# Routing and gathering from the centred input, with the later places made inside the first expert slot

## The reference, cut to what matters

```python
y = jnp.concatenate([mix, xa], -1) @ w_out[i]          # sparse or latent attention, and cross-attention
x = layer_norm(DEEPNORM_ALPHA * x + y, ln_g[i, 0], ln_b[i, 0])
f = hier_moe(x, ...)
x = layer_norm(DEEPNORM_ALPHA * x + f, ln_g[i, 1], ln_b[i, 1])

def layer_norm(x, g, b):
    mu = mean(x); var = mean(square(x - mu))
    return (x - mu) * rsqrt(var + LN_EPS) * g + b

def hier_moe(xs, ...):        # 4 groups of 4 experts, 512 hidden features each
    pg = softmax(xs @ w_grp + b_grp)              # the best group
    le = (xs @ w_exp + b_exp) of that group       # its 4 experts, softmax, the best two
    hdn = silu(xs @ w_gate[e]) * (xs @ w_up[e]) * gate[e]
    return sum over e of hdn @ w_down[e]
```

## Time and profile before

| | |
|---|---|
| median of 3 executions | 2118.57 us (2117.32 to 2120.0) |
| profiled execution | 2114.99 us, span 2113.2 us |
| granted PE clock, mean | 0.996 |
| PE, DVE, ACT busy | 97%, 69%, 53% of the span |

### The profile page before, as it was taken

The page is one execution under the profiler, slowest core; times in us unless marked ns, Lnnn a source line. Parts: engine busy times, 40 slices in busy tenths (PEclk is TensorE's granted clock), DMA queues, the critical chain, the costliest instruction groups (busy, mean ns, idle before and its releaser), DMA issues. The chain is left out here.

```text
span 2113.2 us, 34585 instructions
## 1 busy us (share of the span) xinstructions
PE 2044.1 (97%) x14050; PEld 1853.5 (88%) x14050; DVE 1464.0 (69%) x2157; ACT 1114.7 (53%) x1580; POOL 26.3 (1%) x35
## 2 busy tenths in 40 slices
PE   7999999999999999989999989999999889999998
PEld 7999997999999998879999967888888758888886
DVE  5666785666666665576665477788987466888896
ACT  4333733544343445574333456677775455776774
POOL 1000000000000020000000000000000000000000
PEclk9999999999999999999999999999999999999999
DMA  9555322655545543435553532589985514789992
GB/s 310 186 186 184 123 89 92 211 185 186 186 148 185 185 146 100 154 124 189 186 184 124 156 123 100 204 323 368 351 328 207 220 40 160 271 328 337 343 359 93
DMA packets 246671, 421.44 MB, mean 199 GB/s; under 512 B 7716, under 2 KB 135104, under 8 KB 246432
## 3 DMA queue, kind: packets, MB, share of 16 engines
q1 hardware_dynamic: 245632, 418.09, 56.2%
q0 software_dynamic: 544, 1.62, 0.2%
q10 hardware_dynamic: 384, 0.21, 0.1%
HBM read 416.70 MB, written 1.05 MB: 198 GB/s over the span
## 5 line engine op out<-in xcount | busy, mean ns | idle before, releaser
L662 PE MATMUL banks<-x_hi,w_hi 128*128 128x256 f32 x1360 | 385.8, 284 | 0.0
L663 PE MATMUL banks<-x_lo,w_hi 128*128 128x256 f32 x1360 | 384.9, 283 | 0.0
L664 PE MATMUL banks<-x_hi,w_lo 128*128 128x256 f32 x1360 | 384.8, 283 | 0.0
L3318 DVE TENSOR_TENSOR w_lo<-weight_ring,w_hi 128x1024 fp32r<-128x1024 f32 x256 | 300.3, 1220 | 25.4 <-ACT w_hi L3136 16.9
L608 ACT ACTIVATE w_hi<-weight_ring 128x1024 fp32r<-128x1024 f32 x87 | 92.0, 1057 | 419.3 <-PE banks L664 419.2
L624 DVE TENSOR_TENSOR w_lo<-weight_ring,w_hi 128x1024 fp32r<-128x1024 f32 x88 | 107.7, 1224 | 242.4 <-ACT w_hi L608 242.4
L3136 ACT ACTIVATE w_hi<-weight_ring 128x1024 fp32r<-128x1024 f32 x256 | 256.0, 1053 | 36.0 <-PE banks L2966 20.4
L1084 DVE TENSOR_TENSOR pieces<-weight_ring,pieces 128x512 fp32r<-128x512 f32 (+2 forms) x245 | 167.8, 692 | 144.4 <-ACT pieces L1073 141.9
L662 PEld LDWEIGHTS banks<-x_hi,w_hi 128*128 128x128 f32 x1360 | 261.1, 192 | 0.2
L663 PEld LDWEIGHTS banks<-x_lo,w_hi 128*128 128x128 f32 x1360 | 261.1, 192 | 0.1
L664 PEld LDWEIGHTS banks<-x_hi,w_lo 128*128 128x128 f32 x1360 | 261.1, 192 | 0.0
(11 more groups left out here) (406 smaller groups left out, 4079.8 us busy)
## 6 DMA issues: line engine op xcount, KB each, us to landing
weight_ring<-in_ffn_w_in SPq DMA_DIRECT2D x88, 1024.0 KB, 7.6
weight_ring<-in_moe_w_gate SPq DMA_DIRECT2D x64, 1024.0 KB, 6.6
weight_ring<-in_moe_w_up SPq DMA_DIRECT2D x64, 1024.0 KB, 9.0
weight_ring<-in_moe_w_down SPq DMA_DIRECT2D x48, 1024.0 KB, 11.9
weight_ring<-in_ffn_w_out SPq DMA_DIRECT2D x44, 1024.0 KB, 9.8
weight_ring<-in_moe_w_down SPq DMA_DIRECT2D x8, 2048.0 KB, 11.5
weight_ring<-in_hg_w_in SPq DMA_DIRECT2D x12, 1024.0 KB, 8.2
weight_ring<-in_fox_w_in SPq DMA_DIRECT2D x12, 1024.0 KB, 8.4
```

What stands on the lines that cost most here:

```text
L662: pe.matmul(out, w_hi, m_hi, start=start, stop=False, skip_group_check=True)
L663: pe.matmul(out, w_hi, m_lo, start=False, stop=False, skip_group_check=True)
L664: return pe.matmul(out, w_lo, m_hi, start=False, stop=stop, skip_group_check=True)
L3318: dve.tensor_tensor(self.gate_up_piece(s, p, self.w_lo), self.gate_up_piece(s, p), self.gate_up_piece(s, p, self.w_hi.bitcast(F32)), ALU.s ...
```

## The change

1. **LayerNorm 0 and 2** (`routes`). DVE adds row chunks ahead of PE's mean, so PE sums four tiles in place of eight. The centred input is multiplied by the gain only (`dve_gain`, `act_gain`), and logits and turned tiles are made from that. What is missing is put in later: the shift through the routing weights is eight small products in advance (`pe_shift_routes`), the reciprocal of the root is a column of 128x2 applied to the logits and as ACT's scale on the turned tiles, and the shift is a bias in `act_tokens` and a scalar in `dve_tokens`, one instruction for each 128x128 tile, in every slot.
2. **Places and gates.** The gates of the experts come after the tokens of slot 0, the other places (`dve_spread`, with the plan) after step 1 of slot 0, PE's products with them (`pe_places`) ahead of step 2 of slot 0. The real normalised `k.x` is formed by DVE (`dve_rstd`, `dve_scale`) and ACT (`act_shift`) during steps 3 to 7 of slot 0. The plan is loaded to registers ahead of slot 3.
3. **Weights.** DVE's four first weight pieces stand one in the mixer's output, one ahead of the centring, one after slot 0's places, one between the two halves of the tokens.
4. **SP** counts the unused places as free itself, after waiting for DVE's last release.
5. **LayerNorm 1**: ACT's order of the affine and of the memory rows' copies is turned round.

```diff
 class LayerNorm:
+        if self.routes is not None:
+            self.pe_shift_routes(pe)
         out = b.claim(pe, f"ln_m{i}")[:, 0:T]
+        if self.adds:
+            pe.wait_ge(k.ln_added, self.adds)
+            for kk in range(2):
+                pe.matmul(out, k.ones, k.sq[:, kk], start=kk == 0, stop=False)
+            pe.wait_ge(k.x_ready, 4 * self.before)
+            for kk in (KD - 2, KD - 1):
+                last = pe.matmul(out, k.ones, k.x[:, kk], start=False, stop=kk == KD - 1)
...
+        k.keep_busy(pe, k.psum[:, 0, :], 4)
+        self.pe_sums(pe, 0)
+        self.pe_sums(pe, 1)
+        self.pe_sums(pe, 2)
+        self.pe_logits(pe, 0)
+        b.filled(self.pe_sums(pe, 3), f"ln_v{i}")
+        self.pe_logits(pe, 1)
+        self.pe_logits(pe, 2)
+        for t in range(TT):
+            last = pe.matmul(out[:, t:t + 1], k.std[0:1, t * P:(t + 1) * P], k.ones[0:1, 0:1], start=t == 0, stop=t == 1, skip_group_check=True)
+        b.filled(self.pe_logits(pe, 3), f"ln_lg{i}")
...
     def act(self, act):
-        if self.memory:
-            act.wait_ge(k.x_ready, 4 * self.before)
-            self.memory.act_turned(act)
         for c in range(3):
             act.wait_ge(k.ln_scaled, 4 * i + c + 1)
...
             ins.then_inc(k.x_ready, 1)
+        if self.memory:
+            act.wait_ge(k.x_ready, 4 * self.before)
+            self.memory.act_turned(act)
...
+    def dve_scale(self, dve, c):
+        dve.tensor_tensor(k.x[:, cs], k.x[:, cs], k.rstd[:].unsqueeze(1).to_broadcast([P, 2, T]), ALU.mult).then_inc(k.ln_scaled, 1)
 class Moe:
     def sp(self, eng):
                 eng.sem_inc(r.full[n % SLOTS], self.landed[s])
+                eng.wait_ge(r.free[n % SLOTS], n // SLOTS + 2)
+                eng.sem_inc(r.free[n % SLOTS], self.TURN // SLOTS)
...
+            if s == 2 and i == 0:
+                self.pe_places(pe)
+                pe.wait_ge(sem["places_read"], 4 * self.layer + 4)
...
     def act_tokens(self, act, gather, c):
-        act.activation(self.x_hi[:, 4 * c:4 * c + 4], k.psum[:, 2 + c, :].rearrange("p (k n) -> p k n", n=P),
-                       ACT.Copy).then_inc(sem["xs_hi"], 1)
+        for n in range(4):
+            ins = act.activation(self.x_hi[:, 4 * c + n], k.psum[:, 2 + c, n * P:(n + 1) * P], ACT.Identity, bias=self.norm.shift(4 * c + n))
+        ins.then_inc(sem["xs_hi"], 1)
...
     def dve_tokens(self, dve, gather, c):
-        dve.tensor_tensor(self.x_lo[:, 4 * c:4 * c + 4], k.psum[:, 2 + c, :].rearrange("p (k n) -> p k n", n=P),
-                          self.x_hi[:, 4 * c:4 * c + 4].bitcast(F32), ALU.subtract).then_inc(sem["xs_lo"], 1)
+        for n in range(4):
+            ins = dve.scalar_tensor_tensor(out=self.x_lo[:, 4 * c + n], in0=k.psum[:, 2 + c, n * P:(n + 1) * P],
+                                           scalar=self.norm.shift(4 * c + n), in1=self.x_hi[:, 4 * c + n].bitcast(F32),
+                                           op0=ALU.add, op1=ALU.subtract)
+        ins.then_inc(sem["xs_lo"], 1)
...
+            if i == 0 and s == 1:
+                self.dve_spread(dve)
+            if i == 0 and 3 <= s < 7:
+                if s == 3:
+                    self.norm.dve_rstd(dve)
+                self.norm.dve_scale(dve, s - 3)
```

More of the change, by code:

```diff
@@ new lines, in pe, with pe_shift_routes @@
+        b.filled(last, f"ln_r{i}")
+        b.filled(self.pe_logits(pe, 3), f"ln_lg{i}")
+    def pe_shift_routes(self, pe):
+        k, b, i = self.k, self.k.banks, self.i
+        pe.wait_ge(k.small_ready, k.small_all)
+        out = b.claim(pe, f"ln_c{i}")[:, 0:G_N + E_N]
+        for kk in range(KD):
+            last = pe.matmul(out, self.shift(kk).to_broadcast([P, P]), k.w_route[:, self.routes, kk], start=kk == 0, stop=kk == KD - 1)
+            k.keep_busy(pe, k.psum[:, 0, :], 1, 256)
+        b.filled(last, f"ln_c{i}")
@@ L2777, in __init__ @@
         self.name = name
-        k.banks.plan(*[name + n for n in ("lg", "x0", "x2", "x1", "rank", "x3", "st0", "st1", "st2", "gates")])
+        k.banks.plan(name + "x0", name + "x2", name + "x1", name + "x3", name + "rank")
         self.sem = k.moe
@@ L2920, in pe, with place_bank, pe_places @@
             self.pe_gather(pe, 0, c)
-        pe.wait_ge(sem["spread"], 2 * self.layer + 2)
+        b.wait_read(pe, name + "rank")
+        self.slots(pe, self.pe_slot, self.pe_last_slot, self.pe_skip)
+    def place_bank(self, q):
+        return self.k.psum[:, (6, 7, 1)[q], :]
+    def pe_places(self, pe):
+        k, sem = self.k, self.sem
+        pe.wait_ge(sem["gates"], self.layer + 1)
+        pe.wait_ge(sem["spread"], 2 * self.layer + 2)
+        out = k.psum[:, 0, :]
+        for i in range(self.SLOTS_N):
+            for t in range(TT):
+                last = pe.matmul(out[:, i * E_G:(i + 1) * E_G], self.place[:, t, i * P:(i + 1) * P], self.best[:, t], start=t == 0, stop=t == 1)
+        last.then_inc(sem["places"], 1)
         for q in range(3):
-            out = b.claim(pe, f"{name}st{q}")
+            out = self.place_bank(q)
             for n in range(4 * q, min(4 * q + 4, 2 * self.SLOTS_N)):
@@ L3431, in dve_skip @@
             dve.sem_inc(sem[n], by)
-        for free in k.ring.free:
-            dve.sem_inc(free, self.TURN // SLOTS)
     def pool(self, pool):
```

275 lines of the change are left out of this document (186 added, 89 removed).

## The result

The changed kernel takes 2128.64 us (median of 5 executions, 2127.24 to 2134.55) against 2118.57 for the kernel before (5 executions, 2117.26 to 2123.11): 1.005 times as long, with a 95% interval of 1.0034 to 1.0065. It is slower, by 10.1 us. The profiled execution has a span of 2126.8 against 2113.2, 13.6 more. PE's busy time is the same to 0.3 us (2044.1 before). So what was added is nearly all waiting.

What follows compares the result with a forecast made beforehand. PE's matmuls set the time, with a chain of dependences at the boundaries. Boundaries −2.6, turns +5.4, layer norm 1 +1.9 and clock +1.7 sum to +6.4 on the median 2118.57, giving 2125.0 us, range 2117 to 2130.

Steps and rivals of the forecast that it cites:

- the summed case: Whole kernel: slower as all terms summed, 2125.0 us, its own range 2121.5 to 2128.5; chance 0.45.
- Up to the gather and to the experts: Each boundary: −3.2 us up to the gather and −4.3 from there to the first expert matmul, together −7.5.
- Slot 0: Work moved into slot 0 at each boundary: 3.25 + 0.95 + 1.5 + 0.5 us, against −7.5 ahead of it.
- their reading: Slot 0: PE waits for ACT's reading of three banks and the gates, +0.95 us (0.4 to 2.2).
- the wait for step 1: Slot 0: the gates chain delays DVE's pieces, so PE waits ahead of step 1, +1.5 us (0 to 3.4).
- Forming the input: Slot 0: the reciprocal and four scalings add 4.2 us of DVE work over four steps, costing +0.5 (0 to 2).
- Turns: Turns between slots: longer splits cost 2.7 us per MoE, +5.4 in all (1.0 if short instructions are cheap, up to 8).
- Layer norm 1: Layer norm 1: affine activations ahead of ACT's copies delay PE's products, +1.9 us, and the clock falls after idling, +1.7.
- DVE had no room: Rival for slot 0 and turns: DVE has room and catches up, 2118.1 us, not slower; chance 0.17.
- The clock did fall in layer norm 1: Rival for layer norm 1: the clock does not fall there, +4.7 us, 2123.3; chance 0.15.
- Short instructions weren't cheap: Rival for the turns: short instructions are cheap, turns cost 2.2 in place of 5.4, 2121.8 us; chance 0.10.
- The collision that I had named: Rival: ring place 0, freed later, lands after 1814 and each boundary loses 2 to 4 more, 2131 us; chance 0.05.

Runs made afterwards that it cites:

- e9: Changed kernel with spread, gates, places and their copies ahead of slot 0 again, DVE's weight pieces 2 and 3 in the layer norm; 2129.11 us, ratio 1.005.
- e12: e10 with the normalised input formed by DVE and ACT in slot 1 instead of slot 0; 2116.46 us against 2119.51 for the kernel before, 0.9985.
- e6: Changed kernel with the split in one long instruction in slots 1 to 3, the norm's shift left out there; 2126.68 us, ratio 1.0037 to the kernel before.
- e4: Kernel before with only SP's counting of the unused ring places changed; 2118.41 us against 2119.07, ratio 0.9997.
- e1: Changed kernel with DVE counting the unused ring places as free again, so SP's transfers start later; 2128.79 us, ratio 1.0048 to the kernel before.
- e3: Changed kernel with both SP's count and ACT's order in layer norm 1 undone; 2125.02 us, ratio 1.0033 to the kernel before.
- e10: e9 with layer norm 1 as before the change, long splits in slots 1 to 3, shift added once by DVE; 2116.05 us against 2118.45, 0.9983.
- e7: e3 with the split in one long instruction in slots 1 to 3 and the shift's rows added once by POOL; 2131.7 us, ratio 1.0061 to before.
- e8: e7 with DVE making the gates after the first two weight pieces of step 1 in slot 0; 2128.88 us, ratio 1.0053 to the kernel before.
- e2: Changed kernel with ACT copying the memory rows ahead of the affine activations again; 2125.58 us, ratio 1.0031 to the kernel before.
- e5: Changed kernel run again unedited, on another chip with 8 executions; 2128.07 us, ratio 1.0047 to the kernel before.
- e11: Changed kernel with products of zeros filling PE's two waits in slot 0; 2131.63 us, ratio 1.0055 to the kernel before.

## Why the prediction was right, point by point

The prediction was 2125.0, range 2117 to 2130, slower with 0.6; measured was 2128.64. The sign, the mechanisms and most sizes hold, but one term is missing. Its own sum was +6.4 between two profiled executions. These differ by 13.6, of which 2.3 lie ahead of the first boundary (1311.33 and 1313.64) and −1.5 in the attention, in code that is the same. That leaves 12.8 in the changed parts, twice the sum. The time is only 3.6 above the number because the profiled execution before lay 3.6 below its median and the changed one at its own: profile for profile the forecast was 2121.4 and the measured time 2128.6. That 2128.64 lies inside a range that ends at 2130 is luck in part; it is just above the summed case's own range (to 2128.5).

- *Up to the gather and to the experts*, −7.5 per boundary: measured −7.5 (22.84 for 30.38) and −7.7 (21.21 for 28.94). Right, the 4.6 behind the gather too (4.5).
- *Slot 0*, +6.2: measured +6.4 and +6.3. The terms: places 3.5 for 3.25, their reading 0.80 for 0.95, the wait for step 1 1.13 and 1.16 for 1.5. Forming the input was mis-sized, 1.0 here by the remainder and 1.3 to 1.4 by e9 and e12, for 0.5.
- *Turns*, +5.4: measured +5.5 (2.6 in layer 0, 2.9 in layer 1; 1.7 of each lies between the ends of slot 0 and of slot 2). e6 shows that the splits are the cause of these 1.7; of the third turn's 1.0 to 1.2 PE's second wait is a part, which e6 takes away only from 0.86 to 0.51. Four short ones took 1.14 for the 1.23 that I had.
- *Layer norm 1*, +1.9 and +1.7 for the clock: both appear. From the squares' sums to the products it is 1.8 longer, PE waits 6.55 where I had 6.3, and the products take 1.7 more at the low clock. But ahead of them the sums take 9.7 in place of 3.7. This is the step that failed: "SP's own count of the free places lets the transfer of `mem_w_kv` start earlier by some us, so PE's wait of 3.39 for it (ahead of 1646.81) goes" was taken as free. I asked what the transfers would release and not what they would collide with. The 2.89 of standing and the 3.0 at the clock of 0.52 behind it are the term that is missing, 5.9. e4 shows the stall with SP's part alone, e1 and e3 show it gone without, and the instruction packet that comes 2.2 to 3.3 later is what the transfers delay.
- *What the median shows of it.* All terms come from profiles. Medians give 10.1 for the change, and 4.1 less with both parts of layer norm 1 undone, where the profiles of that stretch give 7.4. The remainder goes with where the clock falls elsewhere (last column, slot 0), which differs from kernel to kernel. What decides that I couldn't settle.
- *The rivals.* DVE had no room: PE's waits at the turns grew as forecast. The clock did fall in layer norm 1. Short instructions weren't cheap. The collision that I had named, ring place 0 landing late, didn't come: PE has no wait on a DMA in the slots; the one that came was at another place. After 6.55 of idle time the clock was 0.52. After 3.39 the sixteen transposes of the trace before took 1.97, at the full clock (that shows it; the stretch from 1650 that the prediction read starts 3.2 later), while in e1, after 3.44, they take 3.62, at a granted clock of 0.53. And after 2.89 the changed kernel's sums had 0.52, after 2.52 e12's had 1.00. So in these runs the length of the idle time alone did not decide it. The rule that the prediction cites from the Trainium skill ("TensorE: Matmul & The Clock Gate", "Why this matters for your kernels"), that idle gaps bring the clock down to half, agrees for the gap of 6.55 and not for the one of 3.39 before.

The Trainium skill ("Runtime: NRT & Kernel Launch", "Instruction fetch mechanics") says that a taken branch to code outside what is loaded makes the engine fetch it by DMA before it goes on. I take the jump over the fifth slot for such a branch, which no row says. The traces agree as far as PE waits there for its sequencer ("PEq": 0.90 in e3, 2.87 in e10, 5.10 in e9) and goes on at a nearly fixed time behind a packet of instructions, which comes later when the DMA engines are full.

## What to carry to other kernels

Work moved off a path of dependences pays only where it lands in slack, and an engine at 69% may have none in the steps in question: read the lead of DVE at the very step, not its share. An instruction that goes from one long to four short (1.14 for 0.60 here) costs that at every turn of a loop, though it was changed for the sake of the first. Starting a transfer earlier isn't free when it fills the DMA engines as an engine needs a packet of instructions: in e4 the stall with the low clock behind it cost 1.8 us more than the earlier weights gave. And read a change of a few us from its stretch as well as from the median, since where the clock falls moves the total by as much.

## What the runs showed of the hardware that was not expected

- PE's standing behind the last slot, its two stops taken together: 0.9 to 1.3 us where the weights' transfers started 2.2 us after the scatter (e1, e3, e7, e8), 3.6 to 5.8 us where they started 5.5 us ahead of it (changed, e2, e4, e5, e6, e9, e11), 2.9 and 2.5 in e10 and e12, with the transfers behind the scatter. The instruction packet comes 2.2 to 3.3 us later behind the early transfers, and but for e3 (one stop, 1.6) the sums go on 2.4 to 3.7 us behind it.
- Two additions of 128x1024 on POOL (5.73 us) made one DVE instruction of 1.22 take 3.15.
- The clock fell in slot 0 in some profiles and not in others: to 0.70 of a stretch with PE busy 8.47 of 9.00 us (e2), to 0.89 with 8.94 (e11), and not at all with 8.19 (changed). A stretch of unchanged code took 53.3 or 54.8 us by it.
